# One layer of a hybrid diffusion backbone: turned blocks, the tiles behind the convolution and attention's last tiles in another order

## The reference, cut to what matters

```python
def trunk_layer(x, cond, lp, attend):
    sh1, sc1, gt1, sh2, sc2, gt2 = ada_mod(cond, lp['w_ada'], lp['b_ada'])
    h = rms_norm(x, lp['norm1_g']) * (1.0 + sc1) + sh1
    q, k, v, hy = split_projection(h @ lp['w_in'])
    att = attend(q, k, v)
    hyo = hyena_mixer(hy, lp)
    merged = jnp.concatenate([rms_norm(att, lp['gnorm_att']), rms_norm(hyo, lp['gnorm_hyena'])], axis=-1)
    x = x + gt1 * (merged @ lp['w_out'])
    h2 = rms_norm(x, lp['norm2_g']) * (1.0 + sc2) + sh2
    x = x + gt2 * hier_moe(h2, lp)
    return x, k, v

def hyena_mixer(hy, lp):
    uc = short_conv(hy, lp['conv_w'], lp['conv_b'])
    x0, x1, v = jnp.split(uc, 3, axis=-1)
    z = (v * x1).astype(f32)
    ...
    y = bidirectional_long_conv(z, h_fwd, h_bwd) + z * lp['hyena_skip']
    return (y * x0).astype(hy.dtype)
```

## Time and profile before

| | us |
|---|---|
| median of 3 runs | 746.22 |
| the three runs | 745.2, 746.22, 746.88 |
| the profiled execution | 746.89 |
| its span in the profile | 745.2 |
| PE busy | 702.1 (94%) |
| DVE busy | 534.5 (72%) |
| ACT busy | 411.5 (55%) |
| POOL busy | 109.5 (15%) |

### The profile page before, as it was taken

How to read it: one execution, slowest core, us unless ns; L and a number is a source line. 1 busy time by engine, 2 the same in 40 slices (tenths; PEclk the granted TensorE clock), 3 DMA queues, 4 the chain that set the end, 5 groups by cost and what they waited for, 6 DMA issues and landing times.

```text
span 745.2 us, 10728 instructions
## 1 busy us (share of the span) xinstructions
PE 702.1 (94%) x3842; PEld 532.2 (71%) x3842; DVE 534.5 (72%) x837; ACT 411.5 (55%) x623; POOL 109.5 (15%) x166
## 2 busy tenths in 40 slices
PE   6889999989999999999999289999999999999994
PEld 2358998949977885555544278888888888888863
DVE  4453716399632135566656989999999999999997
ACT  4755323331233043554543467788888887788833
POOL 3000000000031027554211101111111111111000
PEclk9999999999999999999999599999999999999998
DMA  9991325041399619800039888999999999999663
GB/s 321 416 392 52 121 106 198 22 157 63 142 221 286 228 60 383 224 2 29 29 103 347 290 331 300 365 364 388 373 389 397 382 388 386 376 377 366 235 243 144
DMA packets 81506, 186.26 MB, mean 250 GB/s; under 512 B 9156, under 2 KB 19684, under 8 KB 78260
## 3 DMA queue, kind: packets, MB, share of 16 engines
q1 hardware_dynamic: 73252, 166.64, 61.5%
q0 software_dynamic: 6448, 16.86, 6.7%
q10 hardware_dynamic: 1760, 2.17, 1.0%
HBM read 173.16 MB, written 18.38 MB: 257 GB/s over the span
## 4 chain that ended last, share of the span: by engine, by line
PE 85%; DVE 6%; DMA 4%; ACT 2%; issue 2%; SPq 0%; POOLq 0%; DVEq 0%; ACTq 0%
PE bank L2074 55%; PE bank L1966 13%; PE bank L1975 6%; PE bank L1986 3%; DMA slot<-in_w_ada 2%; PE bank L2235 2%; DMA slot<-in_w_down 2%; PE bank L2213 1%; PE bank L2206 1%; PE bank L2036 1%; DVE big L1904 1%; PE bank L2017 1%; DVE big L1914 1%; DVE big L1909 1%; DMA big<-h_scratch,big 1%
## 5 line engine op out<-in xcount | busy, mean ns | idle before, releaser
L1770 DVE TENSOR_TENSOR WL<-slot,WH 128x1024 fp32r<-128x1024 f32 x188 | 219.2, 1220 | 9.0 <-ACT WH L1223 7.9
L1223 ACT CAST WH<-slot 128x1024 fp32r<-128x1024 f32 x188 | 183.5, 1058 | 2.4 <-PE bank L2074 1.4
L2074 PE MATMUL bank<-WH,xgTh 128*128 128x512 f32 x256 | 102.2, 399 | 3.1 <-DVE xgTl L1762 3.1
L2074 PE MATMUL bank<-hTh,WP 128*128 128x384 f32 (+1 forms) x320 | 99.8, 312 | 1.2 <-DVE hTl L1415 1.2
L2074 PE MATMUL bank<-WH,xgTl 128*128 128x512 f32 x256 | 100.5, 393 | 0.0
L2074 PE MATMUL bank<-hTh,WL 128*128 128x384 f32 (+1 forms) x320 | 98.7, 308 | 0.0
L2074 PE MATMUL bank<-hTl,WP 128*128 128x384 f32 (+1 forms) x320 | 98.7, 308 | 0.0
L2074 PE MATMUL bank<-WL,xgTh 128*128 128x512 f32 x248 | 96.5, 389 | 0.0
L1966 PE MATMUL bank<-slot,big 128*128 128x512 f32 (+1 forms) x224 | 87.7, 539 | 0.1
L1975 PE MATMUL bank<-ident,big 128*128 128x128 f32 x424 | 60.6, 282 | 7.7 <-DMA big<-h_scratch,big 4.8
L1966 PEld LDWEIGHTS bank<-slot,big 128*128 128x128 f32 x224 | 40.9, 190 | 35.1 <-issue 33.1
(11 more groups left out here) (283 smaller groups left out, 1073.4 us busy)
## 6 DMA issues: line engine op xcount, KB each, us to landing
slot<-in_w_down SPq DMA_DIRECT2D x16, 2048.0 KB, 15.5
slot<-in_w_up SPq DMA_DIRECT2D x15, 2048.0 KB, 17.1
slot<-in_w_gate SPq DMA_DIRECT2D x13, 2048.0 KB, 16.0
slot<-in_w_ada SPq DMA_DIRECT2D x12, 2048.0 KB, 11.3
slot<-in_w_in SPq DMA_DIRECT2D x6, 2048.0 KB, 21.2
y_scratch<-dftp SPq DMA_DIRECT2D x1, 5120.0 KB, 35.6
big<-y_scratch SPq DMA_DIRECT2D x10, 512.0 KB, 7.5
slot<-in_w_out SPq DMA_DIRECT2D x2, 2048.0 KB, 15.0
```

The lines of the kernel that those rows point to most:

```text
L1223: act.copy(WH[:, high_half(w, s), r, :], quarter(n, s, w, r)).then_inc(high_ok[w], 1)
L1770: dve.tensor_tensor(quarter_low(n, s, w, r), quarter(n, s, w, r), WH[:, high_half(w, s), r, :].bitcast(F32), ALU.subtract).then_inc(low_ok ...
L2074: ins = pe.matmul(out, l[u], r[v], start=first and i == 0, stop=last and i == 2)
```

## The change

It has four parts. (1) `TURNS_AHEAD` is 4 instead of 6. (2) Behind the convolution the context tile is turned and copied first, PE's context spectrum waits for that copy alone, and ACT does the last two middle taps (x0, blocks 2 and 3) behind the five copies. (3) At the end of attention: the last tile's `o` bank is multiplied straight into attT and squared straight from the bank; tile 2's quarter sums and logits and tile 3's h2 change places with tile 4's `wa` and sums; for h2's tile 4 DVE makes only the gain and the reciprocal, ACT scales the rows by it, and the shift is added in HBM: POOL stores the shift rows (SH2) there in step 9 and at the end adds the scaled rows by a transfer with `accum_op=ALU.add`. SP's store goes. (4) The two semaphores of a result tile become one.

```diff
-LOGITS_AT = {13: 0, 17: 1, 21: 2}
+LOGITS_AT = {13: 0, 17: 1, PAIRS * NT + 2: 2}
-TURNS_AHEAD = 6
+Z_TILES = (CT, *range(CT))
+TURNS_AHEAD = 4
...
-    for t in range(NT):
+    for t in Z_TILES:
         add(("zT", t), "act")
...
+        if v == LATE_STEP + 1:
+            add(("rp", NT - 3), "dve", 0)
...
-            sp.wait_ge(h2_ok, 2 * NT)
-            sp.dma_start(h2_dram[(NT - 1) * P:NT * P, :], h2[:, (NT - 1) % 2, :]).then_inc(last_h2_out, 16)
...
+                if v == ROUTER_STEP:
+                    pool.wait_ge(sh2_in, 32)
+                    pool.dma_start(h2_dram[(NT - 1) * P:NT * P, :], SH2[1]).then_inc(last_h2_out, 16)
...
+            pool.wait_ge(last_scaled, 1)
             pool.wait_ge(last_h2_out, 16)
+            pool.dma_start(h2_dram[(NT - 1) * P:NT * P, :], h2[:, (NT - 1) % 2, :], accum_op=ALU.add).then_inc(last_h2_out, 16)
+            pool.wait_ge(last_h2_out, 32)
...
-                    conv_rest(c, pair)
-            for t in range(NT):
+                    conv_copied(c, pair)
+                    if c == 1 or pair == 0:
+                        conv_tapped(c, pair)
+            for t in Z_TILES:
                 b = full(act, "zT", t)
                 drain(act.copy(zt[:, t, :], b[:, :]), "zT", t)
+            conv_tapped(2, 1)
...
+            act.wait_ge(rows_rooted, 1)
+            act.activation(h2[:, (NT - 1) % 2, :], h2[:, (NT - 1) % 2, :], ACT.Copy, scale=ss[:, 2, NT - 1:NT]).then_inc(last_scaled, 1)
...
+            def last_out_tile(b):
+
+                bk = full(dve, "o", b)
+                drain(dve.tensor_tensor(attT[:, :, b * P:(b + 1) * P], bk[:, :].rearrange("p (a n) -> p a n", n=P),
+                                        chn[:, 2, :].unsqueeze(2).broadcast_to([P, CB, P]), ALU.mult), "o", b)
...
+                if v == LATE_STEP:
+                    root_taken(NT - 2)
+                    for g in range(2):
+                        shifted_half(NT - 2, g)
...
                         scaled_rows(NT - 1)
-                        root_taken(NT - 1)
-                        for g in range(2):
-                            shifted_half(NT - 1, g)
+                        last_root_taken()
                         logits(NT - 2)
...
+                if v == PAIRS * NT:
+                    last_out_tile(b)
+                    dve.wait_ge(wt2_ok, ADDED[("wa", NT - 2, 1)])
+                    scaled_rows(NT - 2)
...
-            for t in range(NT):
+            for t in Z_TILES:
                 b = open_bank("zT", t)
...
-            have(pe, "zT", NT - 1)
...
+            have(pe, "zT", CT)
             context("ufp", (zt[:, CT, :], zt[:, CT, :]))
+            have(pe, "zT", CT - 1)
```

More of the change, by code:

```diff
@@ L126, in add_route @@
             turn[1] += 1
+    def add_route(b):
+        add_turned(b)
         add(("rp", b), "dve", 7)
@@ L510, in program @@
         y_out = [sem("y_out0"), sem("y_out1")]
-        yab_in = [[sem(f"results_in{t}{k}") for k in range(2)] for t in range(NT)]
+        yab_in = [sem(f"results_in{t}") for t in range(NT)]
         f_mul, f_sum, both_ok = sem("sum_gated"), sem("sum_full"), sem("results_added")
@@ L764, in load_results @@
                     for k in range(2):
-                        sp.dma_start(yab[:, t, k], table[:, t, k]).then_inc(yab_in[t][k], 16)
+                        sp.dma_start(yab[:, t, k], table[:, t, k]).then_inc(yab_in[t], 16)
             sp.wait_ge(used[1], (NE - 1) * 4)
@@ L930, in _ @@
                 for t in range(NT):
-                    for k in range(2):
-                        pool.wait_ge(yab_in[t][k], 16)
+                    pool.wait_ge(yab_in[t], 32)
                 pool.wait_ge(f_sum, 2 * NT)
@@ L1031, in conv_input, with conv_copied @@
                     win_high(act, c + 1, cb)
-            def conv_rest(c, pair):
+            def conv_copied(c, pair):
                 two = slice(2 * pair, 2 * pair + 2)
@@ L1039, in conv_rest, with conv_tapped @@
                 drain(act.copy(ustrip[:, two, LAT + 2:LAT + 2 + CTX], b[:, :, P:P + CTX]), "hyp", c, pair)
+            def conv_tapped(c, pair):
                 have(act, "hyp", c, pair)
@@ L1046, in conv_rest @@
                                    bias=cwb[:, HYROW[c], d, 3:4]).then_inc(tap_ok, 1)
+            def conv_rest(c, pair):
+                conv_copied(c, pair)
+                conv_tapped(c, pair)
             odd_half(1, 0)
@@ L1135, in att_squares @@
                 have(act, "o", b)
-                act.activation(osq, oraw[:, b % 2], ACT.Square).then_inc(osq_ok, 1)
+                if b == NT - 1:
+                    raw = bank[JOBS[JOB[("o", b)]][1]][:, :].rearrange("p (a n) -> p a n", n=P)
+                else:
+                    raw = oraw[:, b % 2]
+                act.activation(osq, raw, ACT.Square).then_inc(osq_ok, 1)
             def x1_square(b):
@@ L1649, in _ @@
                 b = v // PAIRS - 1
-                if b == NT - 1 and v % PAIRS == 2:
-                    modulated(b - 1)
                 if v == ROUTER_STEP:
@@ L1841, in both_results @@
             def both_results(t):
-                for k in range(2):
-                    dve.wait_ge(yab_in[t][k], 16)
+                dve.wait_ge(yab_in[t], 32)
                 dve.tensor_tensor(yab[:, t, 0], yab[:, t, 0], yab[:, t, 1], ALU.add).then_inc(both_ok, 1)
@@ L1942, in _ @@
                 for t in range(NT):
-                    for k in range(2):
-                        dve.wait_ge(yab_in[t][k], 32)
+                    dve.wait_ge(yab_in[t], 64)
                 for t in range(NT):
@@ L2290, in mixed @@
                 src, k0 = (attT, 0) if kind == "wa" else (hyoT, CB)
-                if kind == "wa":
+                if f == ("wa", NT - 1, 0):
+                    have(pe, "o", b)
+                elif kind == "wa" and b < NT - 1:
                     pe.wait_ge(att_ok, b + 1)
```

27 lines of the change are left out of this document (18 added, 9 removed).

## The result

The changed kernel took 751.25 us, the median of five runs (749.41 to 752.14), against 746.44 us for the kernel before (745.2 to 746.88, five runs). The ratio is 1.0056, with a 95% interval of 1.0044 to 1.0067: slower by 4.2 us (3.3 to 5.0) by the ratio, 4.8 us by the medians. The forecast was 747.3 us, with a range from 744.4 to 750.4 us. The profiled execution of the changed kernel is the fastest of its five, 749.41 us with a span of 747.7 us; the one of the kernel before, 746.89 us, lies at the slow end of its five. So the two traces differ by 2.5 us where the medians differ by 4.8.

A forecast was written before the change was run, and what follows sets the result against it. The prediction took the chain of waits, over four fifths on PE, as the bound; 0 for four blocks, +1.7 for context and taps, -0.6 at attention's end gave +1.1 us: 747.3 us against the median, range 744.4 to 750.4.

The forecast's parts named there:

- the clock behind PE's wait: At the spectra: half speed for 2.9 us might raise the loss from +1.3 to +2.1 us; the middle, +1.7, was taken.
- the length of the adding transfer: End of attention: h2's last tile, added in HBM, lands 8.1 us after issue, bounds 3.4 and 14 us.
- Four blocks: End of adaLN's first group: four turned blocks ahead instead of six cost 0 us, bounds -0.1 and +0.3.
- The context tile and the taps: Turn from short convolution to spectra: context copied first, two taps behind the copies, +1.7 us, bounds +1.2 and +2.9.
- The wait for bank 0: Behind PE's fourth spectrum: PE stands still 4.8 us until VectorE's third ufp multiply frees the bank.
- bank 3's phase pair: Last spectrum: it can't start before VectorE's first phase pair ends at 161.9 us, giving +1.3 us at full clock.
- The numbers 2.9 us earlier: End of attention: the first gather's indices are ready at 415.2 us instead of 418.1.
- the first rival: End of attention: the adding transfer outlasts the indices; at 10.5 us the kernel is +3.4 us, 749.6 us; chance 0.26.
- The plain store beside loads: End of attention: POOL's plain store of the same tile beside weight loads, 7.0 us, was the adding transfer's base.
- The addition: End of attention: the second read of 0.5 MB at 390 GB/s adds some 1.1 us to the transfer.
- the slow transfer: End of attention: the adding transfer needs over 8.7 us and delays the gather; 749.6 us at 10.5 us, chance 0.26.
- The third rival: At the spectra: the bank is free at 153.8 us, late taps don't hold PE; 741.4 us, chance 0.07.

The follow-up runs named there:

- spare_five: The changed kernel with five spare matmuls between PE's fourth and fifth spectrum, where it stands idle: 749.44 us, ratio 1.0046.
- no_z_order: The changed kernel with z turned in the old order and the two taps ahead of the copies: 747.86 us, ratio 1.0019.
- pairs_first: taps_plain_ufp with VectorE's low parts for q moved behind the two phase pairs of the real half: 741.82 us, ratio 0.9930.
- taps_first: The changed kernel with the last two taps ahead of the five copies, context tile still first: 747.65 us, ratio 1.0012.
- taps_plain_ufp: The changed kernel with taps ahead of the copies, last h2 tile shifted by VectorE and stored plainly, and ufp ahead of the low parts: 743.70 us.
- no_add: The changed kernel with a plain store by POOL in place of the adding transfer, last tile's shift left out: 749.45 us, ratio 1.0044.
- held_load: The changed kernel with SP's 2 MB w_down load held back until the adding transfer has landed: 751.46 us, ratio 1.0061.
- down_last: The changed kernel with SP's 2 MB w_down load held back until the first gather has landed: 747.37 us, ratio 1.0009.
- six_ahead: The changed kernel with six turned blocks ahead again instead of four, nothing else: 751.46 us, ratio 1.0061.

## Why the prediction was wrong

The places and the waits were right. Two terms of the sum were too small: the clock behind PE's wait (+0.4 us, it cost 0.8 to 2.0) and the length of the adding transfer (8.1 us, it took 9.96).

**Four blocks: right.** 0 us was forecast; 23.91 us stand before, and 23.90 to 23.95 in every trace after but the one explained above.

**The context tile and the taps: mechanism right, one term mis-sized.** The wait for bank 0 came as written: 4.54 us, ended by the third multiply, where 4.8 were forecast. The +1.3 us at the full clock, from bank 3's phase pair, is what spare_five measured (+1.28). That it fits so closely is partly luck: VectorE's third multiply came 1.6 instead of 1.9 us late, and the last spectrum took 1.12 instead of 0.86 us. The term that failed is the clock behind the wait. I took +0.4 us, the mean of nothing and of a +0.8 worked out from the 2.8 us that the low clock had lasted before; it cost 0.8 to 2.0 us. No row gave a reason for the "nothing". In the two traces with 2.5 us of idle time in front of the context transform, before and no_z_order, it is 10.17 and 10.45 us from this transform to the adaLN sums, 1.2 and 1.5 us more than in pairs_first with its clock up; and with the 4.54 us the last eight records took 5.17 to 6.36 us in all six traces, against 3.60 for the first eight. Only behind the shorter waits, 1.63 us in taps_first and 1.83 us in taps_plain_ufp, did the clock stay at 1.00. The sum of the part is +2.1 to +3.2 us in the traces and about +3 us in the runs, beyond the bound of 2.9 us in some executions.

**The numbers 2.9 us earlier: right, and a little better.** They are there at 414.7 us in the old frame; 415.2 was forecast. It made no difference, since they had left the chain.

**The adding transfer: the other term that failed.** 8.1 us was forecast and 9.96 measured; this is the first rival's place, at about its price of 10.5. Two sizes were too small. The plain store beside loads was taken at 7.0 us, but at this place, in no_add, it takes 8.3: SP issues a 2 MB load 0.9 us ahead of it, and held_load and down_last show that this load costs the adding transfer 2.3 to 2.8 us. I had named the load and given it no price of its own. The addition was taken at 1.1 us and cost 1.7; by the forecast's own figures, 0.5 MB at 390 GB/s, it is 1.3. The issue was 0.4 us earlier than forecast, so the gather started 1.3 us later than forecast. It also took 0.2 us longer, and the part gave +0.9 instead of -0.6 us.

**Sum.** Forecast 1.7 - 0.6 = +1.1 us. In the changed kernel's own trace it is +2.3 for the first, +0.9 for the second and 0.5 us in the rest, 3.7 us; in six_ahead's, which differs in a part that costs nothing, 3.2, 0.9 and 0.5 us, in all 4.7. The ratio gives 4.2 us. Of the 0.5 us in the rest, 0.25 in the changed kernel's trace stand at `w_ada`, at the start; what lies behind the first gate product has no cause that a run shows, and this last stretch scatters from 318.0 to 319.2 us over the traces without spare matmuls in the routing. The upper bound of the first part and the slow transfer were never added up: together they give 746.2 + 2.9 + 1.7 = 750.8 us, above the range's end of 750.4, though still below the measured median of 751.25 us. The third rival, free banks, did not come with this change. PE did go through all spectra without a wait for a bank in pairs_first, but that kernel has the two taps ahead of the copies again and VectorE's low parts moved. With the late taps no kernel had them moved; by an estimate from the rows, PE's 4.54 us less the low parts' 2.36, it would still stand some 2.2 us.

## What to carry to other kernels

When a wait of PE is removed, follow the next bank back to the engine that empties it, and price the new wait twice: its own length, and the half clock that can follow it, in full where every nearby row shows it. Work taken from a busy engine and given to a transfer is only cheap where the transfer has room: count what is issued just ahead of it, and what the following transfer then meets. Reordering the work on the releasing engine, with nothing removed, was worth 3.6 us by the ratios here, 2.5 us in the traces, about as much as undoing either part that lost.

## What the runs showed of the hardware

- A call of `matmul` in fp32 with 512 columns is two records of 0.43 us at the full clock, 0.87 us together (10 calls: 20 records, 8.75 us). Eight spectra are 16 records.
- Around 4.54 us without work the granted clock fell to 0.50 in all six traces that have them: in the changed kernel's about when PE restarted, at 158 us, until some 161 us; in no_add's and down_last's from 156 us, while PE still stood idle, until past 162 us. With spare matmuls in that time it stayed at 1.00. Behind waits of 1.63 and 1.83 us it stayed at 1.00 too. Why the low stretch differs between executions of one kernel, 5.17 to 6.36 us for the same eight records, was not settled.
- An adding transfer of 512 KB beside weight loads takes 10.0 to 10.3 us (11.0 once), a plain store in its place 8.3, and the adding one without the newest 2 MB load 7.1 to 7.6 us.
- A gather of 128 rows takes 4.2 to 4.5 us behind the loads (5.3 once) and 7.8 us when a 2 MB load is issued 0.9 us ahead of it.
